# Turning attention probabilities with a diagonal of inverted sums instead of scaling and transposing them

## The chip, the cores and the metric

The kernel runs on one core of a Trainium2 chip. The metric is the device time of one execution in microseconds. The core has TensorE (matmul), VectorE, ScalarE, GpSimd and SyncE, each with its own instruction queue in order; they wait for one another with semaphores.

## The reference

Two blocks of a diffusion model run one after the other on 512 tokens and 256 context tokens of width 1024. The change touches the attention of the second block alone. That block has two layers: in the first, attention runs over the 512 tokens and the 256 context tokens, in the second over the 512 tokens alone. There are 8 query heads of 64 channels on 2 heads of keys and values; a query block of 128 tokens sees the 256 context tokens and the blocks beside it.

```python
p = softmax_with_sink(jnp.concatenate([s_ctx, s_loc], axis=-1) * scale, sink).astype(v.dtype)
o = (jnp.einsum('bhgqk,bkhd->bqhgd', p[..., :L], v_ctx)
     + jnp.einsum('bhgqk,bkhd->bqhgd', p[..., L:], vs))
```

The softmax has one more term in its sum, a learned "sink" for each head, which has no value row. All of it is computed in float32.

## The kernel before

The kernel is written with five queues in parallel; each stage has a function for each engine. A semaphore is waited for by a count that a small class (`Tally`) keeps while the program is built, so the order of instructions in a function is the order on its engine.

Attention of one layer goes over items `(c, s, qb)` (`att_items`): c is one of four chunks, each with two heads (s = 0 and 1) whose queries lie in the two halves of the partitions; qb is the query block. The first layer has six query blocks, so 12 items a chunk and 48 in all, with 4, 5, 5, 4, 2 and 2 key blocks of 128 keys (512, 640, 640, 512, 256 and 256 keys). The second has four query blocks, 8 items a chunk and 32 in all, with 4, 5, 5 and 4 key blocks. Items 2p and 2p+1 are pair p: two heads of one query block.

What is done for an item, engine by engine:
- TensorE, `scores(p)` (line 2670): the scores of both heads of a pair, each in a PSUM slot of its own; it waits until the minima of the pair before have emptied the slots.
- VectorE, `top(i)` (line 2813, with a copy of the sink at line 2811 when qb is 0): adds the mask, scales by a negative factor, writes `sl`, and takes the minimum over the keys.
- ScalarE, `expo(i)` (line 2736): the exponential of `sl` into `pr`, and its sum into `small`.
- VectorE, `norm(i)` (lines 2823 and 2825): the reciprocal of the sum, and `pr` times the reciprocal, in place. A reciprocal of line 2823 marks the start of a norm in the trace.
- TensorE, `turn(i)` (line 2681): a transpose of each key block of `pr` into PSUM slot 1; it waits for the norm (`pn_ready`) and for the copy of the item before (`pt_ready`), which empties the slot.
- ScalarE, `copy(i)` (line 2743): the slot into `pT`.
- TensorE, `values(p)` (line 2694): `pT` with the values of both heads, in the two column halves of the array, into PSUM slot 0.

At the end of a chunk `leave` on ScalarE (line 2748) and on VectorE (line 2831) splits the sums of the chunk into two parts.

The order on TensorE is, for each pair p: scores(p+1), turn(2p), values(p-1), turn(2p+1). On ScalarE it is expo(i), copy(i-1). On VectorE it is norm(i), and after each odd i top(i+1) and top(i+2). `pr`, `sl` and the fields of `small` have two places each, taken by i % 2; `pT` has four.

The queries of the last chunk are rotated (rotary embedding) within this loop: TensorE issues the product with the rotation matrix (`pe_rope`, line 2631) at p = 1, and VectorE rotates after norm(3) (`rotate`, lines 2771 to 2780). The scores of the third pair need the PSUM slot that the first instruction of this rotation empties.

Of the kernel before, what the change touches and what calls it, by code (L numbers as in the profile page):

```python
# [25 lines left out]
P = 128  # L26
# [112 lines left out]
def build(nc, ins, out):  # L139
    A = memory_map()  # L140
# [3 lines left out]
    with ExitStack() as ctx:  # L144
        def at(name, shape, words, dt=F32, parts=P):
            t = nc.alloc_sbuf_tensor_at(name, [parts, *shape], dt, offset=base + 4 * words)
            return t

        def fixed(name, shape, dt=F32, parts=P):
            return at(name, shape, A[name], dt, parts)  # L150
# [6 lines left out]
        ident, ones, rot = (fixed(n, [P]) for n in ("ident", "ones", "rot"))  # L157
# [10 lines left out]
        small = fixed("small", [64])  # L168
# [120 lines left out]
        sl = at("sl", [2, 648], A["xx_hi"])  # L289
        pr = at("pr", [2, 648], A["xx_hi"] + 2 * 648)  # L290
        pT = at("pT", [4, 640], A["xx_hi"] + 4 * 648)

        ps = ctx.enter_context(nc.psum_tensor("ps", [P, 4, 1024], F32))

# [2 lines left out]
        def gslot(s):  # L297
            return ps[:, s, :]
# [24 lines left out]
        def semaphore(name):  # L323
            return ctx.enter_context(nc.semaphore(name))
# [78 lines left out]
        pt_done = semaphore("pt_done")  # L403
# [2219 lines left out]
        def key_blocks(qb):  # L2623
            return [b for blocks, _ in key_parts(qb)[0] for b in blocks]
# [9 lines left out]
        def pe_attention(pe, tally, toks):  # L2634
            with_ctx = toks == NT
            pe_rope(pe, tally, hx[:, 6, :], 4)
            pe.wait_ge(slot_free[tally.place("group", 3)], tally.read("group", 3))
            place = tally.place("misc_done")
            pe.wait_ge(misc_free[place], tally.free("misc_done"))
            m = mslot(place)  # L2640
            for c in range(ALLCH):
                last = pe.transpose(m[:, c * P:(c + 1) * P], hx[:, 7, c * P:(c + 1) * P], ident[:, :])
            last.then_inc(misc_done, 1)
            tally.passed("misc_done")
            for c in range(2):
                pe_rope(pe, tally, araw[:, c, :], 2 - c)
            pe_x_tiles(pe, tally, 1, with_ctx)
            for k in range(KC):
                if k == 4:
                    pe_rope(pe, tally, araw[:, 0, :], 1)  # L2650
                pe_x_step(pe, tally, k, with_ctx)
            rotated = tally.n.get("rope_done", 0) + 2
            tally.passed("rope_done", 5)
            items = att_items(toks)

            def scores(p):
                c, _, qb = items[2 * p]
                if qb == 0:
                    pe.wait_ge(rope_done, rotated + c)
                places = []  # L2660
                for _ in range(2):
                    places.append(tally.place("misc_done"))
                    pe.wait_ge(misc_free[places[-1]], tally.free("misc_done"))
                    tally.passed("misc_done")
                parts = key_parts(qb)[0]
                for blocks, col in parts:
                    n = len(blocks) * P
                    for s, place in enumerate(places):
                        r = slice(s * HD, (s + 1) * HD)
                        last = pe.matmul(mslot(place)[:, col:col + n], aq[r, c, qb * P:(qb + 1) * P],  # L2670
                                         akx[r, blocks[0] * P:blocks[0] * P + n], start=True, stop=True)
                        if blocks is parts[-1][0]:
                            last.then_inc(misc_done, 1)

            def turn(i):
                n = len(key_blocks(items[i][2]))
                pe.wait_ge(pn_ready, tally.next("pn_ready"))
                if i >= 1:
                    pe.wait_ge(pt_ready, tally.next("pt_ready"))
                for b in range(n):  # L2680
                    last = pe.transpose(gslot(1)[:, b * P:(b + 1) * P], pr[:, i % 2, 1 + b * P:1 + (b + 1) * P],
                                        ident[:, :])
                last.then_inc(pt_done, 1)
                tally.passed("pt_done")

            def values(p):
                c, _, qb = items[2 * p]
                if qb == 0 and c:
                    pe.wait_ge(mix_ready, tally.next("mix_ready"))
                keys = key_blocks(qb)  # L2690
                for n, kc in enumerate(keys):
                    for s in range(2):
                        f = slice(s * HD, (s + 1) * HD)
                        last = pe.matmul(gslot(0)[f, qb * P:(qb + 1) * P], avt[:, kc, f],
                                         pT[:, (2 * p + s) % 4, n * P:(n + 1) * P], start=(n == 0),
                                         stop=(n == len(keys) - 1), skip_group_check=True)
                if 2 * p + 2 == len(items) or items[2 * p + 2][0] != c:
                    last.then_inc(ao_done, 1)
                    tally.passed("ao_done")

            pe.wait_ge(mix_ready, tally.next("mix_ready", 4))
            scores(0)
            pairs = len(items) // 2
            for p in range(pairs):
                if p == 1:
                    pe_rope(pe, tally, araw[:, 1, :], 1)
                if p + 1 < pairs:
                    scores(p + 1)
                turn(2 * p)
                if p:  # L2710
                    values(p - 1)
                turn(2 * p + 1)
            pe.wait_ge(pt_ready, tally.next("pt_ready"))
            values(pairs - 1)
            pe.wait_ge(mix_ready, tally.next("mix_ready"))
# [47 lines left out]
        def dve_attention(dve, tally, layer, toks):  # L2763
# [34 lines left out]
            items = att_items(toks)  # L2798
            per = len(items) // 4

            def top(i):

                c, s, qb = items[i]
                w = 6 + 8 * (i % 2)
                ms = tally.take("misc_done")
                dve.wait_ge(misc_done, tally.now("misc_done"))
                parts, mask = key_parts(qb)
                n = len(key_blocks(qb)) * P
                sink = mx[:, c + 4 * s, 2:3]
                if qb == 0:  # L2810
                    dve.tensor_copy(sl[:, i % 2, 0:1], sink).then_inc(dve_step, 1)
                    dve.wait_ge(dve_step, tally.next("dve_step"))
                dve.tensor_tensor_reduce(out=sl[:, i % 2, 1:1 + n], in0=mslot(ms)[:, parts[0][1]:parts[0][1] + n],
                                         in1=amask[:, mask * P:mask * P + n], scale=-ATT_SCALE,
                                         scalar=sink, op0=ALU.add, op1=ALU.min,
                                         accum_out=small[:, w + 1:w + 2]).then_inc(misc_free[ms], 1)
                dve.wait_ge(misc_free[ms], tally.read("misc_done"))

            def norm(i):
                n = len(key_blocks(items[i][2])) * P  # L2820
                w = 6 + 8 * (i % 2)
                dve.wait_ge(exp_ready, tally.next("exp_ready"))
                dve.reciprocal(small[:, w + 5:w + 6], small[:, w + 2:w + 3]).then_inc(dve_step, 1)
                dve.wait_ge(dve_step, tally.next("dve_step"))
                dve.tensor_scalar(pr[:, i % 2, 1:1 + n], pr[:, i % 2, 1:1 + n], small[:, w + 5:w + 6], None,
                                  ALU.mult).then_inc(pn_ready, 1)
                dve.wait_ge(pn_ready, tally.next("pn_ready"))

            def leave(c):
                dve.wait_ge(ohi_ready, tally.next("ohi_ready"))  # L2830
                dve.tensor_tensor(mo[1][:, 2 + c, 0:toks], gslot(0)[:, 0:toks], mo[0][:, 2 + c, 0:toks],
                                  ALU.subtract).then_inc(mix_ready, 1)
                dve.wait_ge(mix_ready, tally.next("mix_ready"))
# [2 lines left out]
            top(1)  # L2836
            for i in range(len(items)):
                norm(i)
                if i == 3:
                    rotate(aq[:, 3, :], araw[:, 1, :], toks)  # L2840
                if i % 2 and i + 1 < len(items):
                    top(i + 1)
                    top(i + 2)
                if i > 1 and (i - 1) % per == 0:
                    leave((i - 1) // per - 1)
            leave(3)

        def pe_out2(pe, tally, with_ctx):
# [507 lines left out]
```

## Time and profile before

| | us |
|---|---|
| median of three runs | 3445.23 |
| the three runs | 3444.36, 3445.23, 3453.61 |
| profiled execution | 3453.25 |
| its span in the trace | 3451.5 |
| TensorE busy (matmul), VectorE, ScalarE in it | 3267.9, 1972.7, 1158.8 |

The profile is of one execution. Times of instructions are counted from the start of its span. PE is TensorE's matmul, PEld its weight load, DVE is VectorE, ACT is ScalarE; DVEq is VectorE's sequencer, which takes the waits. A float32 matmul of this kernel leaves two records, with two weight loads; a transpose leaves one. A line of the timeline merges neighbouring records of one line of the program: its second figure is then the time from the start of the first to the end of the last. The granted clock is given as a share of TensorE's full 2.4 GHz. In brackets stands how long the engine had been idle and what released it.

### The profile page before, as it was taken

How to read it: one execution, taken by the hardware profiler on the slowest of the kernel's cores; microseconds unless marked ns; L12 is line 12 of the kernel's file. 1: busy time of each engine (PE TensorE's matmuls, PEld its weight loads, DVE VectorE, ACT ScalarE, POOL GpSimd, SP SyncE). 2: the span in 40 equal slices, each digit the busy share in tenths (PEclk: the TensorE clock that was granted, in tenths of full speed). 3: DMA queues.
4: the chain of work that ended last, by engine and by line, in shares of the span. 5: the costliest groups of instructions: out<-in, count | busy, mean ns of one | idle time of the engine just before them, and what ended most of it. 6: DMA issues, size and time to landing. Idle time of an engine off the chain costs nothing.

```text
span 3451.5 us, 48774 instructions
## 1 busy us (share of the span) xinstructions
PE 3267.9 (95%) x18240; PEld 2848.9 (83%) x18240; DVE 1972.7 (57%) x2920; ACT 1158.8 (34%) x1616; POOL 166.8 (5%) x78
## 2 busy tenths in 40 slices
PE   6999999999999999999999889999999988899998
PEld 3899999888878878887787658999999767578887
DVE  7664442758857668875478565553433467653334
ACT  3421212345531232224343363212212344543223
POOL 7000000000000000000111100000000111000000
PEclk8999999999999999999989999999999989999999
DMA  7333331411132335542210101333322211123222
GB/s 265 121 134 122 131 114 61 146 62 37 38 104 83 105 127 196 189 176 97 74 46 26 74 16 60 134 134 122 134 76 77 76 37 49 38 66 100 91 98 98
DMA packets 102045, 339.09 MB, mean 98 GB/s; under 512 B 10407, under 2 KB 21543, under 8 KB 100488
## 3 DMA queue, kind: packets, MB, share of 16 engines
q1 hardware_dynamic: 83276, 300.96, 25.3%
q10 hardware_dynamic: 18620, 36.11, 2.9%
q8 instruction: 98, 1.61, 0.2%
q14 instruction: 51, 0.42, 0.0%
HBM read 322.88 MB, written 14.16 MB: 98 GB/s over the span
## 4 chain that ended last, share of the span: by engine, by line
PE 79%; DVE 11%; ACT 5%; issue 3%; DMA 1%; ACTq 0%; DVEq 0%; POOL 0%; SPq 0%; POOLq 0%
PE ps L438 63%; PE ps L484 5%; PE ps L468 1%; PE ps L1109 1%; ACT pr L2736 1%; PE ps L2129 1%; PE ps L1057 1%; PE ps L2116 1%; DVE u_ex L1255 1%; DVE u_Z L1369 1%; ACT pT L2743 1%; ACT wr_hi L535 1%; PE ps L1533 1%; PE ps L2670 1%; DVE wr_lo L545 0%
## 5 line engine op out<-in xcount | busy, mean ns | idle before, releaser
L535 ACT ACTIVATE wr_hi<-raw 128x1024 fp32r<-128x1024 f32 x388 | 411.8, 1061 | 599.3 <-PE ps L438 548.6
L545 DVE TENSOR_TENSOR wr_lo<-raw,wr_hi 128x1024 fp32r<-128x1024 f32 x348 | 426.2, 1225 | 79.9 <-ACT wr_hi L535 48.8
L915 DVE TENSOR_TENSOR ff_raw<-ps,ff_gate 128x768 f32<-128x768 f32 (+1 forms) x88 | 72.6, 825 | 580.6 <-PE ps L438 577.7
L438 PE MATMUL ps<-xx_hi,wr_hi 128*128 128x512 f32 x992 | 393.4, 397 | 1.1 <-ACT ff_gate L867 1.0
L438 PE MATMUL ps<-xx_lo,wr_hi 128*128 128x512 f32 x992 | 389.5, 393 | 0.0
L438 PE MATMUL ps<-xx_hi,wr_lo 128*128 128x512 f32 x992 | 389.2, 392 | 0.0
L438 PE MATMUL ps<-xa_hi,wr_hi 128*128 128x384 f32 x1344 | 341.1, 334 | 0.4 <-ACT ff_gate L867 0.4
L438 PE MATMUL ps<-xa_lo,wr_hi 128*128 128x384 f32 x1344 | 341.0, 334 | 0.0
L438 PE MATMUL ps<-xa_hi,wr_lo 128*128 128x384 f32 x1344 | 340.9, 334 | 0.0
L593 DVE CUSTOM_DVE_ANT_0 ps<-raw,cb 128x1024 f32<-128x1024 f32 x240 | 295.3, 1231 | 44.7 <-DMA raw<-in_mod_stream 26.4
L438 PE MATMUL ps<-hid_hi,wr_hi 128*128 128x384 f32 (+1 forms) x1056 | 316.2, 353 | 3.6 <-DVE H L976 1.9
L438 PE MATMUL ps<-hid_lo,wr_hi 128*128 128x384 f32 (+1 forms) x1056 | 315.6, 352 | 0.0
L438 PE MATMUL ps<-hid_hi,wr_lo 128*128 128x384 f32 (+1 forms) x1056 | 315.5, 352 | 0.0
L438 PEld LDWEIGHTS ps<-xa_hi,wr_hi 128*128 128x128 f32 x1344 | 242.5, 188 | 1.0 <-issue 1.0
L438 PEld LDWEIGHTS ps<-xa_lo,wr_hi 128*128 128x128 f32 x1344 | 242.7, 188 | 0.0
L438 PEld LDWEIGHTS ps<-xa_hi,wr_lo 128*128 128x128 f32 x1344 | 242.6, 188 | 0.0
L874 ACT ACTIVATE hid_hi<-ff_raw 128x768 f32 (+1 forms) x88 | 65.2, 740 | 508.7 <-DVE ff_raw L915 508.6
L2966 POOL TENSOR_TENSOR wr_lo<-raw,wr_hi 128x1024 fp32r<-128x1024 f32 x40 | 96.4, 2412 | 2757.2 <-ACT wr_hi L535 2757.2
L438 PEld LDWEIGHTS ps<-xx_hi,wr_hi 128*128 128x128 f32 x992 | 188.0, 189 | 43.3 <-issue 4.1
L438 PEld LDWEIGHTS ps<-xx_hi,wr_lo 128*128 128x128 f32 x992 | 187.6, 189 | 40.5
L438 PEld LDWEIGHTS ps<-xx_lo,wr_hi 128*128 128x128 f32 x992 | 187.7, 189 | 40.1 <-issue 0.8
L438 PEld LDWEIGHTS ps<-hid_hi,wr_hi 128*128 128x128 f32 x1056 | 193.2, 188 | 19.6 <-DVE hid_lo L922 2.6
(426 smaller groups left out, 5370.6 us busy)
## 6 DMA issues: line engine op xcount, KB each, us to landing
raw<-in_stream SPq DMA_DIRECT2D x392, 512.0 KB, 3.4
raw<-in_mod_stream SPq DMA_DIRECT2D x160, 512.0 KB, 4.2
hyena_k<-fst ACTq DMA_DIRECT2D x18, 256.0 KB, 5.1
hK<-hyena_k ACTq DMA_DIRECT2D x4, 1152.0 KB, 6.6
h_kept<-H ACTq DMA_DIRECT2D x2, 2048.0 KB, 8.9
cb<-in_cb ACTq DMA_DIRECT2D x3, 1024.0 KB, 6.5
H<-in_h ACTq DMA_DIRECT2D x1, 3072.0 KB, 12.9
h_kept<-H ACTq DMA_DIRECT2D x1, 3072.0 KB, 11.7
```

The lines of the kernel that those rows point to most:

```text
L438: last = pe.matmul(gslot(slot)[:, col:col + n], w, rhs[part], start=(bi == 0 and pi == 0), stop=(bi == len(blocks) - 1 and pi == 2))
L468: last = pe.matmul(gslot(slots[t])[:, col:col + n], w, rhs[part], start=(k == 0 and pi == 0), stop=(k == steps - 1 and pi == 2))
L484: last = pe.matmul(gslot(slot)[:, col:col + n], w, rhs[part], start=(k == 0 and pi == 0), stop=(k == KC - 1 and pi == 2))
L535: act.activation(wr_hi[:, s, :], raw[:, s % RAW, :], ACT.Copy).then_inc(tile_hi, 1)
L545: dve.tensor_tensor(wr_lo[:, s, :], raw[:, s % RAW, :], wr_hi[:, s, :], ALU.subtract).then_inc(tile_lo, 1)
L593: ins = dve.tensor_tensor_reduce(out=product, in0=tile, in1=factors[:, v, :], scale=1.0, scalar=0.0, op0=ALU.mult, op1=ALU.add, accum_out= ...
L874: act.activation(hid[0][:, bass.ds(i * 2 + q, 1), 0:n], ff_raw[:, q:q + 1, 0:n], ACT.Copy).then_inc(hhi_ready, 1)
L915: dve.tensor_tensor(parts(ff_raw[:, q, :], with_ctx), gparts(slot, with_ctx), parts(ff_gate[:, q, :], with_ctx), ALU.mult).then_inc(slot_f ...
L1057: last = pe.matmul(m[:, j * NX + c * HD:j * NX + (c + 1) * HD], Z[r, c * CH:(c + 1) * CH], queries[r, c * per:(c + 1) * per, 0 if bw else ...
L1109: last = pe.matmul(m[:, j * NX + c * HD:j * NX + (c + 1) * HD], Z[r, c * CH:(c + 1) * CH], queries[r, c * per:(c + 1) * per, 0 if bw else ...
L1255: dve.tensor_tensor(x, cum, a, ALU.subtract).then_inc(ex_in, 1)
L2966: nc.gpsimd.tensor_tensor(wr_lo[:, s, :], raw[:, s % RAW, :], wr_hi[:, s, :], ALU.subtract).then_inc(tile_lo, 1)
```

## The change

A tile `turner` (two places of 128 columns) is added. For each item VectorE no longer multiplies the probabilities; it multiplies the identity matrix by the reciprocals, which gives a diagonal matrix. TensorE no longer transposes each key block of `pr`: it multiplies it with the diagonal, as a float32 matmul with `pr` as the stationary operand, which gives the block transposed and scaled. Before VectorE overwrites a place of the diagonal it waits until the turning two items before is done. VectorE's order becomes norm(i), top(i+2) for every i, and the rotation of the last chunk stands behind norm(2). The orders of TensorE and ScalarE stay.

```diff
+        turner = at("turner", [2, P], A["xx_hi"] + 4 * 648 + 4 * 640)
...
                 for b in range(n):
-                    last = pe.transpose(gslot(1)[:, b * P:(b + 1) * P], pr[:, i % 2, 1 + b * P:1 + (b + 1) * P],
-                                        ident[:, :])
+                    last = pe.matmul(gslot(1)[:, b * P:(b + 1) * P], pr[:, i % 2, 1 + b * P:1 + (b + 1) * P],
+                                     turner[:, i % 2, :], start=True, stop=True, skip_group_check=True)
...
             def norm(i):
-                n = len(key_blocks(items[i][2])) * P
                 w = 6 + 8 * (i % 2)
                 dve.wait_ge(exp_ready, tally.next("exp_ready"))
                 dve.reciprocal(small[:, w + 5:w + 6], small[:, w + 2:w + 3]).then_inc(dve_step, 1)
                 dve.wait_ge(dve_step, tally.next("dve_step"))
-                dve.tensor_scalar(pr[:, i % 2, 1:1 + n], pr[:, i % 2, 1:1 + n], small[:, w + 5:w + 6], None,
+                if i >= 2:
+                    dve.wait_ge(pt_done, tally.next("pt_done"))
+                dve.tensor_scalar(turner[:, i % 2, :], ident[:, :], small[:, w + 5:w + 6], None,
                                   ALU.mult).then_inc(pn_ready, 1)
...
             for i in range(len(items)):
                 norm(i)
-                if i == 3:
+                if i == 2:
                     rotate(aq[:, 3, :], araw[:, 1, :], toks)
-                if i % 2 and i + 1 < len(items):
-                    top(i + 1)
+                if i + 2 < len(items):
                     top(i + 2)
                 if i > 1 and (i - 1) % per == 0:
                     leave((i - 1) // per - 1)
+            tally.passed("pt_done", 2)
             leave(3)
```

## Rows read from the trace of the kernel before

**Rows 1.** The page, busy time of the engines over the span.
```profile
PE 3267.9 (95%) x18240; PEld 2848.9 (83%) x18240; DVE 1972.7 (57%) x2920; ACT 1158.8 (34%) x1616; POOL 166.8 (5%) x78
```

**Rows 2.** Table by stretch: busy us (records) of each engine, clock, DMA, GB/s.
```profile
core 0: us, PE busy (x) PEld busy (x) DVE busy (x) ACT busy (x) POOL busy (x), PEclk, DMA share, GB/s
1951.30:1962.90 11.60, 5.97 (x28) 3.23 (x27) 7.84 (x20) 6.54 (x12) 2.35 (x1) 0.85 0.73 287
...
1990.40:2014.10 23.70, 18.95 (x174) 13.07 (x174) 17.42 (x51) 16.98 (x38) 0.00 (x0) 1.00 0.01 2
...
2952.00:2958.00 6.00, 4.97 (x16) 2.37 (x12) 3.69 (x10) 3.04 (x6) 0.10 (x1) 0.50 1.03 395
...
2981.10:3027.50 46.40, 36.73 (x362) 27.05 (x362) 31.17 (x84) 32.77 (x63) 0.00 (x0) 1.00 0.01 1
```

**Rows 3.** Timeline of VectorE, first reciprocal of a chunk (two chunks).
```profile
1990.48 0.16 DVE L2823 RECIPROCAL small<-small 128x1 f32<-128x1 f32 x1 [0.19 <-ACT pr L2736]
...
2014.11 0.16 DVE L2823 RECIPROCAL small<-small 128x1 f32<-128x1 f32 x1 [0.19 <-ACT pr L2736]
...
2981.14 0.16 DVE L2823 RECIPROCAL small<-small 128x1 f32<-128x1 f32 x1 [0.19 <-ACT pr L2736]
...
2998.88 0.16 DVE L2823 RECIPROCAL small<-small 128x1 f32<-128x1 f32 x1 [0.19 <-ACT pr L2736]
```

**Rows 4.** Timeline of all engines, a pair with 640 keys: start, length, instruction.
```profile
2013.08 0.83 ACT L2736 ACTIVATE pr<-sl,small 128x641 f32<-128x641 f32 x1 [0.79 <-DVE small L2813]
...
2014.03 0.76 PEld L2670 LDWEIGHTS ps<-akx,aq 64*128 64x128 f32 x8 [1.06 <-issue]
2014.04 0.70 ACT L2743 ACTIVATE pT<-ps 128x640 f32<-128x640 f32 x1
...
2015.12 0.53 PEld L2681 LDWEIGHTS ps<-ident,pr 128*128 128x128 f32 x5 [0.33 <-DVE pr L2825]
...
2015.79 0.16 DVE L2823 RECIPROCAL small<-small 128x1 f32<-128x1 f32 x1 [0.94 <-ACT pr L2736]
2015.82 1.07 PEld L2694 LDWEIGHTS ps<-pT,avt 128*64 128x64 f32 x20 [0.17 <-issue]
2015.99 0.70 ACT L2743 ACTIVATE pT<-ps 128x640 f32<-128x640 f32 x1 [0.30 <-PE ps L2681]
2015.99 0.55 DVE L2825 TENSOR_SCALAR pr<-pr,small 128x640 f32<-128x640 f32 x1
2016.58 0.75 DVE L2813 CUSTOM_DVE_ANT_0 sl<-ps,amask,mx 128x512 f32<-128x512 f32 x1
2017.07 0.53 PEld L2681 LDWEIGHTS ps<-ident,pr 128*128 128x128 f32 x5 [0.17 <-issue]
```

**Rows 5.** Instructions by line: duration ns min/median/max, first and last start, forms.
```profile
L2681 PE MATMUL ps<-ident,pr x320: 272/273/474, 1956.9 to 3023.8; 128*128 128x128 f32 x160
...
L2825 DVE TENSOR_SCALAR pr<-pr,small x80: 354/490/1192, 1955.0 to 3022.7; 128x512 f32<-128x512 f32 x32, 128x640 f32<-128x640 f32 x32, 128x256 f32<-128x256 f32 x16
...
L2822 DVEq EVENT_SEMAPHORE  x80: 21/21/21, 1954.7 to 3022.4; - x80
```

**Rows 6.** Timeline of TensorE's matmuls at the blocks with 256 keys.
```profile
1997.32 0.66 PE L2681 MATMUL ps<-ident,pr 128*128 128x128 f32 x4
...
1999.01 0.41 PE L2681 MATMUL ps<-ident,pr 128*128 128x128 f32 x2
1999.35 1.09 PE L2694 MATMUL ps<-pT,avt 128*64 128x128 f32 x16
2000.37 0.44 PE L2681 MATMUL ps<-ident,pr 128*128 128x128 f32 x2
```

**Rows 7.** Timeline of an earlier stage: full-array float32 products of 128 columns.
```profile
772.75 0.39 PE L1074 MATMUL ps<-u_P,vtok 128*128 128x128 f32 x2
...
772.98 0.39 PE L1077 MATMUL ps<-u_eq,u_S 128*128 128x128 f32 x2
```

**Rows 8.** Timeline of another stage: twenty such products in a row.
```profile
1007.78 4.73 PE L2116 MATMUL ps<-hu,dft 128*128 128x128 f32 x40 [0.85 <-DVE hu L2187]
```

**Rows 9.** Timeline of VectorE, scaling of 256 columns.
```profile
2002.72 0.36 DVE L2825 TENSOR_SCALAR pr<-pr,small 128x256 f32<-128x256 f32 x1
```

**Rows 10.** Timeline of TensorE at the start of the second layer's attention.
```profile
2953.06 1.11 PE L2681 MATMUL ps<-ident,pr 128*128 128x128 f32 x4
```

## The prediction

> **What bounds the kernel now.** I read the page from the top. TensorE is busy 95% of the span, but the change touches only attention, and a mean over the span says nothing of a stretch [rows 1]. The stretches table comes next: attention runs twice, from 1951.3 to 2054.0 us and from 2947.8 to 3027.5 us. In a settled chunk of the first stage TensorE is busy 18.95 of 23.70 us, VectorE 17.42, ScalarE 16.98, so there no engine is the bound. In 2952 to 2958 us TensorE's clock was granted at 0.50, its lower level [rows 2]. The time of a chunk (one c: 6 query blocks with 22 key blocks in the first stage, 4 with 18 in the second) is the distance of its first reciprocals: 2014.11 less 1990.48 is 23.63 us, and 2998.88 less 2981.14 is 17.74 us [rows 3].
>
> The timeline of one pair of heads with 640 keys shows the loop: minima of the next head, exponential (at 2013.08), read of its sum, copy of the head before (2014.04), exponential of the other head, its reciprocal (2015.79), scaling, the next minima (2016.58). VectorE and ScalarE hand each other the work. TensorE's idle time lies ahead of the scores (1.06 us before 2014.03), because they wait for both minima [rows 4]. So the loop of VectorE and ScalarE is the limit today, and TensorE has about 5 us to spare in each chunk.
>
> **TensorE's part of the change.** Each key block of 128 columns is turned by a matmul with a diagonal in place of a transpose; there are 320 of them [rows 5]. Price of a transpose: from the start of a turning to the start of the values behind it is 0.70 us with five blocks (2015.12 to 2015.82) [rows 4] and 0.34 to 0.37 us with two (1999.01 to 1999.35) [rows 6]; over three blocks that is 0.111 to 0.12 us each, I take 0.111, and 0.15 us stays as a gap. Price of the matmul: values with 20 records run 1.25 us to the next turning [rows 4], with 16 records 1.02 us (1999.35 to 2000.37) [rows 6]: 0.222 us a key block, and a gap of 0.14 us. There two halves of the array share the time. For the whole array the nearest rows are f32 products of 128x128 by 128 columns in another stage, which follow each other at 0.22 us, two records each [rows 7]. I take 0.222 us: 0.111 us more a block, 35.5 us of TensorE in all. Bounds: 0.111 us (no dearer) and 0.229 us (a run of forty such records takes 4.73 us; less the 0.27 us of the last, over 39, 0.114 us a record) [rows 8].
>
> The Trainium skill (TensorE: Matmul & The Clock Gate, glossary of the tensor engine) calls its transpose mode four times faster for FP32. The rows show twice. Four times the transpose's measured 0.111 us would be 0.444 us a block and a further 71 us of TensorE; the products of [rows 7] run at half of that, so the rows decide.
>
> **VectorE's part.** Scaling 640, 512 and 256 columns takes 0.55, 0.49 (the median) and 0.36 us [rows 4, 5, 9]; the slope of about 0.52 ns a column gives 0.29 us for the 128 columns of the diagonal. Saved: 0.27, 0.20 and 0.07 us on 32, 32 and 16 heads, 16 us of VectorE [rows 5]. Bounds: nothing saved on the 512 form (0.49 us) and 0.29 us.
> The new wait of VectorE, for the product of two heads before, has behind it the diagonal and the minima of the next but one head. It never binds: the exponential of head i stands on ScalarE behind the copy of head i-2, which waited for that same product. 76 met waits cost at the most their 21 ns each, as the one ahead of the reciprocal does [rows 5], 1.6 us on an engine with slack.
> The minima alternate now, so head i+2's stand right behind head i's scaling, and ScalarE gets work sooner. In return, norm(i) of an odd i stands behind minima that wait for the scores of the next pair. The rotation goes from i = 3 to i = 2; it waits for the rope product, which TensorE issues behind the second turning.
>
> **The sum.** I followed the three queues on paper: an instruction starts when its engine is free and what it waits for is done, with the durations above (behind scores a gap of 0.20 us, since the turning follows scores of 4 x 0.222 us after 1.09; the copy starts some 0.33 us behind the last column of a turning) [rows 4]. For the order of today this gives chunks of 23.61 and 17.78 us, against 23.63 and 17.74 read [rows 3], so it may be used for the new order.
> TensorE's own work in a new chunk: scores, two turnings and values are 4 x 0.222 = 0.889 us a key block; gaps are 0.20 + 0.15 + 0.14 + 0.15 = 0.64 us a pair.
> First stage: 22 x 0.889 + 6 x 0.64 = 23.4 us. It still waits 1.84 us, all around the blocks with 256 keys: 0.32 + 0.21 + 0.27 + 0.06 us for the copy that empties the turned slot, 0.55 us for a norm queued behind minima, 0.43 us for minima ahead of the scores. Chunk: 25.23 us, 1.60 more than 23.63.
> Second stage: 18 x 0.889 + 4 x 0.64 = 18.56, waits 0.11: 18.67 us, 0.93 more than 17.74.
> So TensorE becomes the bound, and what VectorE saves lies beside it: 16 us gained there are worth nothing.
> Three settled chunks a stage: 3 x 1.60 + 3 x 0.93 = 7.6 us.
> Ends: behind the last chunk boundary all is in series; the turnings of the second stage's end have 18 blocks, 18 x 0.111 = 2.0 us; the first stage followed the same way gives 2.05. Together 4.1 us.
> Starts: at full clock the new order gives 0.1 us back in each. With the first two turnings at the lower clock, as now in the second stage (four transposes take 1.11 us at 2953.06 [rows 10] against 0.66 later [rows 6]), they cost 1.8 us, since the rope product and the scores stand behind them. In the second stage the lower clock covers them, in the first only part [rows 2]: I take 1.2 and 0.2 us, 1.4 together.
> Sum: 7.6 + 4.1 + 1.4 = 13.1 us. The profiled execution took 3453.25 us (span 3451.5), so it would take 3466.3; it lies 8.0 us above the median of the runs shown, 3445.23, and by that the median goes to 3458.3 us. 0.3% is 10.3 us, about what a measurement of this kernel can tell from no change.
>
> **The rivals.** (A) The forecast, TensorE as bound, 3458 us. Its own bounds: with half of the gaps between TensorE's groups (the column halves need no drain behind a product) the settled sum falls by 6.6 us, to 3452; with 0.229 us a block and both starts wholly at the lower clock it is 3461, and with gaps a third longer on top 3466. Own range 3451 to 3466.
> (B) The same mechanism, but short of 0.3%: the low end of A, or a start that costs nothing. The second stage's waits of only 0.11 us speak against much less; that the sum is a small difference of large numbers, and that the runs of the kernel before are 9 us apart, speaks for it. 3452 us.
> (C) Faster: the product costs no more than the transpose (0.111 us a block). Then the loop of VectorE and ScalarE stays the limit and the shorter norm and the alternation pay: the same queues give stages that are 8.8 and 7.9 us shorter, 3428 us. It decides by the price of a block: at 0.167 us the stages are still 1.6 and 2.8 us faster, and at about 0.18 us the change is neutral. Against it: the two records of [rows 7] for each f32 product where a transpose has one.
> (D) The clock. The skill says on the same page (Part 4, PE-mode transpose) that transposes don't bring the clock gate to full rate; by that rule products in their place would raise the clock. The profile shows 1.00 over both stages once they have settled, though a quarter of TensorE's 174 records in the chunk are transposes (44) [rows 2]. What is left is the low stretch of 6 us in the second stage and 3 to 4 us in the first: if products ended it at once, the starts would cost nothing and give back some 2 us: 3455 us. It is no more than the low half of A.
> (E) The diagonal doesn't get cheap: norm stays at 0.49 us as for 512 columns. 1.6 us more, 3460: inside A, since TensorE hides it.
>
> **How the numbers follow.** A 0.54 (with E), B 0.30, D 0.04 (it falls within 0.3%), C 0.09; 0.03 for something not seen that costs over 0.7%. Faster by over 0.3% 0.09, within 0.3% 0.34, slower 0.57. The predicted time is A's, 3458 us. The range leaves out C and the unseen one and holds A and B with the spread of the runs: 3443 to 3468 us.
>
> **What would show it.** In the changed profile: turnings with two records a block, values 1.26 us after the start of a turning of five blocks; TensorE busy over 95% of a settled chunk in the second stage; chunks of 25.2 and 18.7 us by the reciprocals; VectorE's 128-column form near 0.29 us; idle time of VectorE longer and ended by the scores or the exponential; no wait that a turning of two heads before ends at the diagonal. The prediction is wrong if a turning of five blocks takes under 0.9 us, if TensorE still idles over 2 us in a chunk of the second stage, or if the gap behind a turning is gone.

## The result, and the profile of the changed kernel

| | before | changed |
|---|---|---|
| median of seven runs, us | 3452.48 | 3464.33 |
| lowest to highest | 3444.36 to 3453.64 | 3457.54 to 3470.45 |
| span of the profiled execution | 3451.5 | 3461.9 |
| ratio of the runs | | 1.0041, 95% interval 1.0026 to 1.0057 |

The change makes the kernel slower by 0.41%, some 14 us by the means, from which the ratio is formed, and 12 us by the medians. The seven runs of the kernel before have a median 7 us above that of the first three, so the changed kernel's absolute time lies 6 us above the 3458 us of the prediction, and inside its range.

The first thing to look at is the group of the turnings and that of the diagonal, by line; the columns are those of [rows 5].

```profile
L2682 PEld LDWEIGHTS ps<-turner,pr x640: 186/191/333, 1950.6 to 3032.7; 128*128 128x128 f32 x160
L2682 PE MATMUL ps<-turner,pr x640: 275/275/580, 1950.6 to 3032.8; 128*128 128x128 f32 x160
...
L2827 DVE TENSOR_SCALAR turner<-ident,small x80: 285/286/989, 1949.5 to 3030.7; 128x128 f32<-128x128 f32 x80
...
  DVE small L2823: 0.9, 3
  PE ps L2682: 0.3, 1
...
L2826 DVEq EVENT_SEMAPHORE  x76: 21/21/21, 1953.5 to 3030.5; - x76
```

There are 640 records of turnings where [rows 5] has 320: two for each block. The diagonal takes 0.286 us in the median. The 76 new waits show 21 ns each. The two indented lines are the idle time of VectorE ahead of the diagonal. In one of 80 heads, at 1973.07 us, it is put down to a turning, but the turning that this head waits for, that of two heads before, had begun at 1970.71 us and the values had followed it at 1971.33; three idle times of the same length are put down to the reciprocal. So the new wait costs nothing.

The timeline of all engines over a pair with 640 keys answers to [rows 4]:

```profile
1984.71 0.83 ACT L2737 ACTIVATE pr<-sl,small 128x641 f32<-128x641 f32 x1
1984.83 1.19 PEld L2682 LDWEIGHTS ps<-turner,pr 128*128 128x128 f32 x10 [0.17 <-issue]
...
1985.74 0.16 DVE L2823 RECIPROCAL small<-small 128x1 f32<-128x1 f32 x1 [0.75 <-ACT pr L2737]
...
1986.14 0.73 PEld L2671 LDWEIGHTS ps<-akx,aq 64*128 64x128 f32 x8
...
1987.21 1.19 PEld L2682 LDWEIGHTS ps<-turner,pr 128*128 128x128 f32 x10 [0.33 <-issue]
...
1987.42 0.75 DVE L2814 CUSTOM_DVE_ANT_0 sl<-ps,amask,mx 128x512 f32<-128x512 f32 x1 [1.20 <-PE ps L2671]
...
1988.52 1.07 PEld L2695 LDWEIGHTS ps<-pT,avt 128*64 128x64 f32 x20
1988.69 0.71 ACT L2744 ACTIVATE pT<-ps 128x640 f32<-128x640 f32 x1 [0.72 <-PE ps L2682]
...
1989.76 1.19 PEld L2682 LDWEIGHTS ps<-turner,pr 128*128 128x128 f32 x10 [0.17 <-issue]
```

Turning, scores, turning, values, turning: each starts where the one before ends. A turning of five blocks takes 1.31 us to its successor (1984.83 to 1986.14, 1987.21 to 1988.52); it took 0.70 us. Now the others wait for TensorE: VectorE 1.20 us for the scores, ScalarE 0.72 us for the turning. The 1.06 us that TensorE waited ahead of the scores in [rows 4] are gone.

The table by stretch has one chunk of the first stage and one of the second (columns as in [rows 2]). The last line is the kernel before in a chunk of its second stage.

```profile
1985.74:2011.41 25.67, 24.12 (x219) 18.84 (x218) 15.23 (x51) 16.91 (x37) 0.00 (x0) 1.00 0.00 1
2985.31:3004.23 18.92, 18.86 (x179) 15.23 (x178) 11.21 (x36) 12.76 (x25) 0.00 (x0) 1.00 0.01 2
```

```profile
2981.14:2998.88 17.74, 14.71 (x142) 10.72 (x142) 13.09 (x35) 12.76 (x26) 0.00 (x0) 1.00 0.01 2
```

In the second stage TensorE is busy 18.86 of 18.92 us, where it was 14.71 of 17.74. VectorE fell from 13.09 to 11.21 us, and that bought nothing.

The lengths by the reciprocals of line 2823, as in [rows 3]: start is the first to the fifth, then three chunks, and end is from the last chunk boundary to the end of VectorE's last instruction of the stage. All in us.

| | start | chunks | end | sum |
|---|---|---|---|---|
| before, first stage | 12.06 | 23.65, 23.63, 23.60 | 16.26 | 99.20 |
| changed | 10.73 | 25.67, 25.67, 25.68 | 18.79 | 106.54 |
| before, second stage | 12.14 | 17.76, 17.74, 17.74 | 10.83 | 76.21 |
| changed | 12.21 | 18.93, 18.92, 19.08 | 13.15 | 82.29 |

Attention grew by 7.34 + 6.08 = 13.4 us between these two executions. The spans differ by 10.4 us only, since the first stage began earlier in the changed one: its first reciprocal is at 1949.34 us, against 1954.77. Nothing before it had been changed.

### The profile page after: what moved, and what is told of

The parts are those of the page before. It is cut to its first block, busy times and chain, and to the rows that moved or that the text cites. A ratio compares the mean times of both kernels' runs of the same rounds, so it can differ in the third digit from the quotient of the medians.

```text
span 3461.9 us, 49490 instructions
## 1 busy us (share of the span) xinstructions
PE 3302.2 (95%) x18560; PEld 2887.7 (83%) x18560; DVE 1957.0 (57%) x2920; ACT 1158.7 (33%) x1616; POOL 166.8 (5%) x78
## 4 chain that ended last, share of the span: by engine, by line
PE 83%; DVE 11%; ACT 3%; issue 2%; DMA 1%; ACTq 0%; DVEq 0%; SPq 0%
PE ps L439 63%; PE ps L485 5%; PE ps L2682 2%; PE ps L469 2%; PE ps L1110 1%; PE ps L2695 1%; PE ps L2671 1%; PE ps L2130 1%; PE ps L1058 1%; PE ps L2117 1%; DVE u_ex L1256 1%; DVE u_Z L1370 1%; PE ps L1534 1%; PE ps L2358 1%; DVE xx_lo L792 1%
```

## The experiments

Theory 1 is that of the prediction: a float32 product occupies TensorE twice as long as a transpose, TensorE becomes the bound, and what VectorE does lies beside it. Theory 2 is that the loss comes from VectorE's new order. In the tables, "chunks" is a settled chunk of the first and of the second stage (one behind the first of its stage, with the clock at 1.00 throughout), and "attention" the sum over both stages from the first reciprocal, against 175.4 us before.

**The four that take the change apart.** The old order with the product; the order alone; the diagonal with transposes; more work on VectorE.

Old order, product and diagonal kept:

```diff
-                if i == 2:
+                if i == 3:
                     rotate(aq[:, 3, :], araw[:, 1, :], toks)
-                if i + 2 < len(items):
+                if i % 2 and i + 1 < len(items):
+                    top(i + 1)
                     top(i + 2)
```

> The changed kernel with VectorE's old order (both minima of a pair behind the odd head's norm, rotation behind norm(3)); the product with the diagonal and the short norm stay. Theory 1 (TensorE is the bound, at 0.227 us a key block and a gap of 0.19 us behind a turning): the order hardly matters; chunks of about 25.6 and 19.1 us, attention 1 to 2 us longer than in the changed kernel, the time 14 to 17 us above the kernel before. Theory 2 (the alternation costs: an odd head's norm is queued behind minima that wait for scores): undoing it brings the time back to the kernel before or below, with chunks under 23.6 and 17.7 us.

Order alone: the same lines turned round, in the kernel before.

> The kernel before with VectorE's new order alone: transposes and the scaling in place stay. Theory 1: with transposes TensorE has room, the alternation gives ScalarE its work sooner: chunks of 22.3 and 16.2 us, attention 11.6 us shorter, ratio about 0.9966. Theory 2: chunks longer than before, the time up to 10 us above the kernel before.

Diagonal made, blocks transposed:

```diff
-                    last = pe.matmul(gslot(1)[:, b * P:(b + 1) * P], pr[:, i % 2, 1 + b * P:1 + (b + 1) * P],
-                                     turner[:, i % 2, :], start=True, stop=True, skip_group_check=True)
+                    last = pe.transpose(gslot(1)[:, b * P:(b + 1) * P], pr[:, i % 2, 1 + b * P:1 + (b + 1) * P],
+                                        ident[:, :])
```

> The changed kernel with transposes in place of the product; the diagonal is still made but not used, so the probabilities stay unscaled in the output. It differs from the changed kernel by the price of a block alone (0.111 for 0.227 us). Theory 1: chunks of 21.5 and 15.5 us, attention 17 us shorter than before and 30 us shorter than in the changed kernel, ratio about 0.995. Theory 2 (order and wait cost): no faster than the kernel before.

More work on VectorE, in `norm` of the changed kernel:

```diff
+                dve.tensor_scalar(pT_spare[:, :], amask[:, 0:256], small[:, w + 5:w + 6], None,
+                                  ALU.mult).then_inc(dve_step, 1)
+                dve.wait_ge(dve_step, tally.next("dve_step"))
```

> The changed kernel with one more scaling of 256 columns on VectorE in each norm, between the reciprocal and the wait for the product (its result is not used): 80 x 0.39 = 31 us more work on VectorE, about twice what the change saved there. Theory 1: nearly all of it hides beside TensorE: chunks of 26.5 and 19.4 us, 4 us in all above the changed kernel. A theory in which VectorE's loop still counts: 15 to 31 us above it.

| | chunks, us | attention, us | ratio to before (95%) |
|---|---|---|---|
| changed kernel | 25.67, 18.92 | 188.8 | 1.0041 (1.0026 to 1.0057) |
| old order, product | 25.72, 18.93 | 197.7 | 1.0058 (1.0043 to 1.0073) |
| order alone | 22.29, 16.10 | 167.3 | 0.9975 (0.9964 to 0.9985) |
| diagonal, transposes | 21.47, 15.58 | 157.8 | 0.9949 (0.9932 to 0.9967) |
| changed, more on VectorE | 26.54, 19.21 | 195.7 | 1.0054 (1.0038 to 1.0071) |

The table by stretch, one chunk of each stage, for the old order, then for the diagonal with transposes, then for more work on VectorE:

```profile
1994.25:2019.97 25.72, 24.10 (x219) 18.84 (x217) 15.23 (x51) 16.91 (x37) 0.00 (x0) 1.00 0.00 1
2991.31:3010.24 18.93, 18.86 (x179) 15.24 (x177) 11.21 (x36) 12.75 (x25) 0.00 (x0) 1.00 0.01 2
```

```profile
1981.25:2002.72 21.47, 18.73 (x174) 12.88 (x174) 15.23 (x52) 16.92 (x38) 0.00 (x0) 1.00 0.01 2
2961.63:2977.21 15.58, 14.75 (x142) 10.77 (x143) 11.21 (x36) 12.77 (x26) 0.00 (x0) 1.00 0.00 1
```

```profile
1998.45:2024.99 26.54, 24.19 (x219) 18.85 (x218) 19.49 (x63) 16.92 (x37) 0.00 (x0) 1.00 0.00 1
2994.27:3013.49 19.22, 18.93 (x179) 15.33 (x178) 14.04 (x44) 12.75 (x25) 0.00 (x0) 1.00 0.01 2
```

Theory 2 falls twice. Undoing the order leaves the settled chunks where they were, and the order alone makes the kernel before faster, by 0.25%. Against the changed kernel, the third differs by the instruction on TensorE and by nothing else; its chunks are 4.2 and 3.3 us shorter. One head's turnings of five blocks take 0.61 us less (0.70 for 1.31), 0.122 us a block; over the 44 and 36 blocks that both heads have in a chunk that is 5.4 and 4.4 us of TensorE. Not all of it comes back, since the loop of VectorE and ScalarE is the limit again: TensorE is busy 18.73 of 21.47 us. VectorE is busy for the same 15.23 and 11.21 us in both. In the fourth VectorE works 4.26 us more in a chunk of the first stage and 2.83 us more in one of the second, and the chunks grow by 0.87 and 0.29 us: four fifths and nine tenths of it are hidden. In the first stage TensorE had waits left, around the 256-key blocks, and this may be why it hides less; it was not followed in the trace. Attention grew by 6.9 us where 4 were expected; 3.0 us of it are the first stage's start (13.75 us for 10.73), where the clock was low for 6.8 us.

The expected sizes of the settled chunks were met to 0.2 us. The times were not met as well. The old order with the product came out at 20 us above before by the ratio, not 14 to 17. Its attention is 8.9 us longer than the changed kernel's: 7.6 us of that lie in the starts, 15.82 and 14.71 us where the changed kernel has 10.73 and 12.21, and 1.5 us in the first chunk of each stage (26.60 and 19.46 us). The stretch rows of the old order show what stands beside it in the first stage:

```profile
1954.00:1967.00 13.00, 10.76 (x45) 7.53 (x45) 6.41 (x16) 4.11 (x8) 0.00 (x0) 0.50 0.53 224
```

The granted clock was 0.50 of 2.4 GHz, that is 1.2 GHz, for these 13 us; the changed kernel's was at 1.00 throughout its first start. The order alone was to give 0.9966 and gave 0.9975, with 8.1 us less attention for 11.6 expected. Its starts, 12.79 and 11.77 us, gave nothing (12.06 and 12.14 before), with the clock low for 10.2 and 6.8 us, and the clock fell once more within a chunk, which took 23.36 us for 22.3.

**Half of the heads, and a shorter product.** These ask whether the price of a block is additive, and whether it is the float32 type that costs.

Even head by product, odd head scaled in place and transposed:

```diff
-                    last = pe.matmul(gslot(1)[:, b * P:(b + 1) * P], pr[:, i % 2, 1 + b * P:1 + (b + 1) * P],
-                                     turner[:, i % 2, :], start=True, stop=True, skip_group_check=True)
+                    src = pr[:, i % 2, 1 + b * P:1 + (b + 1) * P]
+                    if i % 2:
+                        last = pe.transpose(gslot(1)[:, b * P:(b + 1) * P], src, ident[:, :])
+                    else:
+                        last = pe.matmul(gslot(1)[:, b * P:(b + 1) * P], src, turner[:, i % 2, :], ...)
...
```

> The changed kernel, new order, but only the even head of each pair is turned by the product with a diagonal; the odd head is scaled in place and transposed as before. Theory 1 (TensorE's price of a block decides, and it is additive): half of the extra TensorE work goes; chunks of 23.8 and 17.4 us, between the order alone (22.3 and 16.1) and the changed kernel (25.7 and 18.9); the time about that of the kernel before, within 4 us. A theory in which the switch between product and transpose costs TensorE a drain: chunks near the changed kernel's.

Probabilities and diagonal as float32r:

```diff
-        pr = at("pr", [2, 648], A["xx_hi"] + 2 * 648)
...
-        turner = at("turner", [2, P], A["xx_hi"] + 4 * 648 + 4 * 640)
+        turnr = at("turner", [2, P], A["xx_hi"] + 4 * 648 + 4 * 640, F32R)
+        prr = at("prr", [2, 648], A["xx_hi"] + 2 * 648, F32R)
...
+                    last = pe.matmul(gslot(1)[:, b * P:(b + 1) * P], prr[:, i % 2, 1 + b * P:1 + (b + 1) * P],
+                                     turnr[:, i % 2, :], start=True, stop=True, skip_group_check=True)
...
```

ScalarE's exponential writes `prr` and VectorE's scaling of the identity writes `turnr`; nothing else differs from the changed kernel.

> The changed kernel with the probabilities and the diagonal stored as float32r, so that each block's product is of that type; the low bits of the probabilities are left out. Where the product of a block takes one record of about the length of a transpose's (0.111 us), theory 1 gives chunks of 21.5 and 15.5 us and 17 us less than before; at 0.06 us a block 20.6 and 15.1 us. If such a short product costs as much as the float32 one (0.22 us), chunks stay at 25.7 and 18.9 us.

| | chunks, us | attention, us | ratio to before (95%) |
|---|---|---|---|
| half of the heads | 23.74, 17.24 | 176.9 | 0.9999 (0.9987 to 1.0011) |
| float32r | 21.50, 15.58 | 165.0 | 0.9995 (0.9986 to 1.0004) |

Half of the heads gives chunks of 23.74 and 17.24 us, for 23.8 and 17.4 expected. The rows of one chunk of each stage, first with half of the heads, then with the order alone, show TensorE's share:

```profile
1994.32:2018.06 23.74, 21.41 (x196) 15.87 (x196) 16.32 (x51) 16.92 (x38) 0.00 (x0) 1.00 0.01 2
2976.81:2994.05 17.24, 16.75 (x160) 12.98 (x160) 12.15 (x35) 12.75 (x26) 0.00 (x0) 1.00 0.01 2
```

```profile
2009.91:2032.20 22.29, 18.88 (x172) 12.99 (x172) 17.42 (x52) 16.93 (x38) 0.00 (x0) 1.00 0.00 1
2973.72:2989.82 16.10, 14.82 (x140) 10.71 (x140) 13.10 (x35) 12.77 (x26) 0.00 (x0) 1.00 0.01 3
```

TensorE is busy for 21.41 and 16.75 us; half way between the order alone and the changed kernel (24.12 and 18.86 us) would be 21.50 and 16.84. So the price is additive. In the second stage TensorE idles 0.49 us in the whole chunk, with eight turnings of alternating kind in it, which leaves little room for a cost of changing between product and transpose.

The float32r product is the surprise. Two lines of its timeline show a turning of five blocks with five records, followed by the values after 0.70 us, as with the transposes of [rows 4]:

```profile
2032.60 0.63 PEld L2682 LDWEIGHTS ps<-turner,prr 128*128 128x128 f32 x5 [0.47 <-DVE turner L2827]
...
2033.30 0.85 PEld L2695 LDWEIGHTS ps<-pT,avt 128*64 128x64 f32 x16
```

Its chunks are as short as with transposes and the cheap diagonal, 21.5 and 15.6 us. But the time did not move: 0.9995, where the transposes gave 0.9949. Some 16 us had got lost again. The profile is of the fastest of the eleven runs (3440.91 us, where the median is 3449.12) and shows part of it: the start of the first stage takes 12.69 us, for 9.36 with transposes, and its first chunk 27.57 us, for 21.68. The rows of that stretch are first the float32r kernel's, and then those of the kernel with diagonal and transposes, over the same number of microseconds:

```profile
1953.00:1976.00 23.00, 21.19 (x102) 15.41 (x102) 11.69 (x35) 10.23 (x20) 0.02 (x1) 0.50 0.34 145
```

```profile
1950.00:1973.00 23.00, 19.13 (x166) 12.81 (x166) 17.25 (x53) 16.11 (x38) 1.31 (x1) 1.00 0.38 152
```

102 records at half clock against 166 at the full one. Whether this is chance or belongs to the kernel was the next question.

**The same kernels once more.** Second profiled executions, unchanged, of the changed kernel, the kernel before, the diagonal with transposes, the float32r product and the order alone.

> The changed kernel unchanged, a second profiled execution: whether the lengths of the two starts depend on the kernel or on chance. Theory 1: settled chunks again at 25.7 and 18.9 us within 0.1; if the clock at the start is chance, the first stage's start (first to fifth reciprocal, 10.73 us in the first profile) differs by up to some us.

> The kernel before unchanged, a second profiled execution: settled chunks again at 23.6 and 17.7 us within 0.1; if the clock at the start is chance, the starts (12.06 and 12.14 us in the first profile) differ by up to some us.

> The kernel with the diagonal made and transposes kept, a second profiled execution (probabilities unscaled in the output, as in the first). It gained about 18 us, the float32r product none in the median although its settled chunks are as short (21.5 and 15.6 us). Theory A (the lower clock at the start is chance, the same for both): the clock of the first attention's start may be low here too, costing some us. Theory B (products in place of transposes bring the low stretch): full clock again, start within 0.5 us of 9.36.

> The kernel with the float32r product, a second profiled execution (low bits of the probabilities left out, as in the first). In the first the clock stayed at 0.50 for over 20 us from the start of the first attention, which cost it some 9 us (start 12.69 us, first chunk 27.57). Theory A (chance): this execution may well show a short low stretch, and then the chunk is 21.5 us. Theory B (tied to this kernel): again over 10 us at 0.50 and a first chunk over 24 us.

> The kernel with the new order alone, a second profiled execution. In the first the clock fell for some 3 us within a settled chunk, which took 23.36 us for 22.3. If such falls are chance, they lie elsewhere or are absent here, and undisturbed chunks are again 22.3 and 16.1 us.

"Low clock" is the time that the granted clock was at 0.50 from the first reciprocal (or up to 0.3 us ahead of it) to the end of the first chunk, for the first and the second stage, read from a table by stretch in steps of 1 us. The last three kernels have one profiled execution.

| | starts, us, first and second execution | low clock, us | settled chunks again |
|---|---|---|---|
| before | 12.06, 12.14; then 13.48, 12.25 | 3.4, 6.8; then 10.2, 6.8 | 23.62, 17.74 |
| changed | 10.73, 12.21; then 12.28, 12.18 | 0, 3.4; then 3.4, 3.4 | 25.68, 18.92 |
| diagonal, transposes | 9.36, 11.47; then 9.36, 10.56 | 0, 6.8; then 0, 3.4 | 21.47, 15.57 |
| float32r | 12.69, 9.26; then 12.65, 13.76 | 23.9, 0; then 23.9, 27.3 | 21.49, 15.58 |
| order alone | 12.79, 11.77; then 12.79, 11.71 | 10.2, 6.8; then 10.2, 6.8 | 22.28, 16.10 |
| old order, product | 15.82, 14.71 | 13.6, 6.8 | |
| changed, more on VectorE | 13.75, 12.25 | 6.8, 3.4 | |
| half of the heads | 14.14, 11.72 | 10.2, 3.4 | |

Settled chunks repeat to 0.03 us wherever the clock is at 1.00. The first start of before and of changed moves by 1.4 and 1.6 us from one execution to the next, so there the length of the low clock is a matter of chance. With float32r it looks otherwise: in three of its four starts the clock fell and stayed low for 23.9 us or more, in none of the 22 other starts for more than 13.6. The second execution has the same long stretch in the first stage (start 12.65, first chunk 27.71 us) and one in the second stage as well, where the first had none:

```profile
1959.00:1982.00 23.00, 21.19 (x108) 15.49 (x107) 11.38 (x36) 10.53 (x21) 0.00 (x0) 0.50 0.30 128
2948.00:2975.00 27.00, 24.96 (x118) 17.99 (x120) 13.12 (x39) 11.81 (x25) 1.22 (x1) 0.50 0.27 98
```

With transposes the second execution runs the same stretch at 1.00 again:

```profile
1949.00:1972.00 23.00, 19.13 (x166) 12.79 (x166) 17.34 (x54) 16.12 (x37) 1.24 (x1) 1.00 0.37 152
```

In that kernel, though, the clock did not fall there at all, so it cannot say how soon it would have risen again. The order alone, also with transposes, can: its clock fell 1.4 us behind the first reciprocal (with float32r 1.1 and 1.4 us behind it) and was back at 1.00 after 10.2 us, in both executions. Its rows:

```profile
1960.00:1962.00 2.00, 2.00 (x11) 1.25 (x7) 1.02 (x3) 0.00 (x0) 0.00 (x0) 0.50 0.27 104
1962.00:1964.00 2.00, 2.00 (x21) 1.60 (x20) 1.66 (x6) 1.57 (x3) 0.00 (x0) 0.73 0.00 0
1964.00:1966.00 2.00, 2.00 (x17) 1.38 (x15) 1.11 (x3) 1.52 (x4) 0.00 (x0) 1.00 0.00 0
```

The float32r kernel's, first execution, of the time when its TensorE had filled up again:

```profile
1962.00:1964.00 2.00, 2.00 (x16) 1.88 (x17) 1.84 (x6) 1.13 (x2) 0.00 (x0) 0.50 0.01 4
...
1974.00:1976.00 2.00, 2.00 (x14) 1.88 (x16) 1.43 (x6) 1.32 (x4) 0.00 (x0) 0.50 0.03 8
```

All seven rows of 2 us from 1962 to 1976 have TensorE busy for 2.00 us and the clock at 0.50. TensorE's busy time does not set the two kernels apart.

The timed runs agree. The mean granted clock over the span was 0.963 to 0.969 in the eleven float32r runs, and 0.967 to 0.974 in the six with transposes. And with the order alone the fall within a chunk came in a settled chunk again, 23.38 us for 23.36, here in the second execution:

```profile
2001.00:2004.00 3.00, 2.96 (x11) 1.88 (x12) 1.12 (x3) 0.81 (x2) 0.00 (x0) 0.54 0.00 0
```

So the float32r kernel gives back at its starts much of what its chunks gain: 7.2 us of attention against the transposes in the first pair of profiles, 19.2 in the second. Why its clock stays low so long was not found out. It is not the length of TensorE's idle time alone: both kernels, and the order alone, wait the same 2.55 us ahead of the second pair's scores.

The version that beats both kernels is the order alone, with 3443.6 us in the median of twelve runs, 0.25% under the kernel before. The kernel with diagonal and transposes is shorter still, but it leaves the scaling out.

## Why the prediction was right, step by step

- **A product costs twice a transpose, two records a block.** Right: 640 records. The pace is (1.31 - 0.65) / 3 = 0.22 us a block (two blocks take 0.65 us to the values, 1999.73 to 2000.38), for 0.222 taken, and what stays behind a turning is 0.20 us where I took 0.15 from the transposes. A turning of five blocks has 1.31 us, not the 1.26 that were forecast.
- **The Trainium skill's factor of four for the transpose mode** (TensorE: Matmul & The Clock Gate, glossary). The measurement decides against it: two, in this kernel. And a product in float32r is no dearer than a transpose.
- **TensorE becomes the bound.** Right: 99.7% busy in a chunk of the second stage. (The 5 us that it was said to have to spare in each chunk were 4.75 us in the first stage and 3.0 in the second, 17.74 less 14.71.) In the first 94%, with the waits where they were put: 0.31 us for the copy at 1992.09, 0.20 at 1996.39, 0.39 us for the norm queued behind minima at 2001.42 (0.55 forecast), 0.36 us ahead of the scores at 2002.50 (0.43) and 0.25 at 2005.78 (0.27), as the timeline of TensorE of the changed kernel shows:

```profile
1992.09 1.13 PE L2682 MATMUL ps<-turner,pr 128*128 128x128 f32 x8 [0.31 <-ACT pT L2744]
...
1996.39 0.68 PE L2682 MATMUL ps<-turner,pr 128*128 128x128 f32 x4 [0.20 <-ACT pT L2744]
...
1999.73 0.71 PE L2682 MATMUL ps<-turner,pr 128*128 128x128 f32 x4
2000.38 0.66 PE L2695 MATMUL ps<-pT,avt 128*64 128x128 f32 x8
2001.42 0.71 PE L2682 MATMUL ps<-turner,pr 128*128 128x128 f32 x4 [0.39 <-DVE turner L2827]
2002.50 1.35 PE L2671 MATMUL ps<-akx,aq 64*128 64x384 f32 x8 [0.36 <-DVE small L2814]
...
2005.78 1.13 PE L2682 MATMUL ps<-turner,pr 128*128 128x128 f32 x8 [0.25 <-ACT pT L2744]
```

- **Chunks.** 25.23 and 18.67 us were forecast, 25.67 and 18.92 measured. What was too small is the gap behind the turnings: 12 and 8 turnings by 0.05 us are 0.6 and 0.4. In the first stage the waits, 1.5 us for 1.84 forecast, took 0.3 of it back. Settled part: 9.8 us, not 7.6.
- **Ends.** 4.1 us forecast, 2.53 + 2.32 = 4.9 measured.
- **Starts.** 1.4 us forecast, -1.3 and +0.1 measured in the first pair of profiles; in the second pair -1.2 and -0.1. This was the weakest term. I had priced the first two turnings at the lower clock as before, but how long the clock is low differs between executions and kernels. Its error of 2.7 us cancelled most of the 3.0 us that chunks and ends came out above. The sum, 13.1 us, met the 13.4 us of both pairs of profiles; that it did so to 0.3 us is luck, for without this cancelling it would have been 3 us off.
- **VectorE's saving.** The diagonal takes the forecast 0.29 us and VectorE saves 1.9 us in a chunk of the second stage; little or nothing of that is worth anything beside the product. The experiment with 4.26 us more on VectorE shows the cover, and its limit: 0.87 us came through.
- **The new wait never binds.** Right.
- **Rival C, the product at the price of a transpose.** It did not come, but its time can be read: the diagonal with transposes has 17.6 us less attention, for 16.7 forecast.
- **Rival D, products raise the clock.** Its starts were to give some 2 us back, and they gave 1.3 us in both pairs of profiles, so D had the starts better than A; the chunks and ends made the time A's. At the start of the second stage the clock was low for 3.4 us in both executions of the changed kernel and for 6.8 us in both of the kernel before. But that the products did this isn't shown: in the first stage the old order with products had 13.6 us and the diagonal with transposes none, and with float32r products the clock stayed low longest. The Trainium skill's sentence that transposes don't bring the clock gate to full rate (TensorE: Matmul & The Clock Gate, Part 4) can't be tested here on transposes alone, since they are only a quarter of the records; in the first stage the clock rose after 10.2 us with that quarter of transposes, in the order alone, and after 23.9 us with float32r products in their place.
- The 0.25% that the order alone gives was in the queues that I followed for C, but I had not asked what each part is worth by itself. Asked ahead of its run, the same queues gave the order alone 11.6 us less attention (measured: 8.1 us). Beside the product the order has nothing to give in the settled chunks, since TensorE is the bound there; the 8.9 us between old and new order with the product lie in starts and first chunks, where the clock was low for 13.6 us in the first stage against none, and how much of that is chance isn't known.

## What to carry to other kernels

Before work is moved onto an engine that idles, add up that engine's work within the stretch of the change with its gaps. Here TensorE had 3 to 5 us to spare in a chunk and was given 4 to 5, and a bound of hand-overs between two engines became a bound of one. Then price each part of a change alone: the order gained 8 us, the diagonal in place of the long scaling would have gained 9.5 more with transposes (167.3 to 157.8, 3.7 of it in the starts, where the clock had its part), and the product cost 31 (157.8 to 188.8). An estimate by following the queues instruction by instruction is good to some tenths of a us in a settled loop, and poor at its start, where the clock isn't settled.

## What the runs showed of the hardware that was not expected

- A 128x128 block turned by a float32r product takes one record, and five take 0.70 us to the next group, the same as five transposes; five float32 products take 1.31 us.
- Once the granted clock had fallen at the start of a stage, it stayed at 1.2 GHz for 23.9, 23.9 and 27.3 us with float32r products, TensorE busy all the time in the last 14 us and more of each stretch; in the other kernels, with transposes or float32 products, it stayed for 3.4 to 13.6 us. Against the diagonal with transposes this kernel's attention was 7 and 19 us longer in the two pairs of profiles, and its ratio to the kernel before is 16 us worse. The cause is open.
- The fall of the clock within a chunk of the order-alone kernel came at the same place in two executions (1.1 us longer each time), so such a fall can belong to a kernel as well as to chance.
